# Sums of squares as moving tiles on four column quarters, turned afterwards; one product for the delta layer's two gates, and its key norm ahead of the last convolution

## The reference

```python
# hybrid mixer (layer "ssd"): two norms ahead of its output projection
ssd_out = grouped_rmsnorm(y * silu(z), ssd_norm, 2)        # 2 groups of 512 channels
sc_out  = grouped_rmsnorm(sc, sc_norm, 16)                 # 16 groups of 64 channels
return concatenate([ssd_out, sc_out], axis=-1) @ w_out
# delta rule (layer "gdn"): 4 query heads and 4 key heads of 128 channels
qkv = silu(causal_conv(qkv, conv_w))
q, k, v = split(qkv, [4 * 128, 8 * 128], axis=-1)
q = repeat(l2_norm(q), 2) * 128 ** -0.5;  k = repeat(l2_norm(k), 2)
beta = sigmoid(b);  g = -exp(a_log) * softplus(a + dt_bias)  # a, b: 8 + 8 columns of xn @ w_in
# then chunks of 64 tokens: decays exp(g_i - g_j), inverses of unit lower triangles, a state per head
```

## Time and profile before

| What | Value |
|---|---|
| median of 3 runs | 1317.17 us (1316.4 to 1320.26) |
| profiled execution | 1317.74 us, span 1316.0 us |
| TensorE busy | 1083.5 us, 82% of the span |
| VectorE busy | 638.3 us, 49% |
| ScalarE busy | 438.7 us, 33% |
| GpSimd busy | 8.4 us, 1% |
| chain of waits, by engine | PE 61%, DMA 27%, DVE 5%, ACT 4% |
| mean granted clock of TensorE | 0.944 |
| experts, 250 to 700 us | DMA busy share 1.01, 402 GB/s |

### The profile page before, as it was taken

The page is one execution under the profiler, slowest core; times in us unless marked ns, Lnnn a source line. Parts: engine busy times, 40 slices in busy tenths (PEclk is TensorE's granted clock), DMA queues, the critical chain, the costliest instruction groups (busy, mean ns, idle before and its releaser), DMA issues.

```text
span 1316.0 us, 18871 instructions
## 1 busy us (share of the span) xinstructions
PE 1083.5 (82%) x7678; PEld 792.5 (60%) x7678; DVE 638.3 (49%) x1245; ACT 438.7 (33%) x689; POOL 8.4 (1%) x32
## 2 busy tenths in 40 slices
PE   5999988895656656655656899999989989899998
PEld 5999967731211212121212789887768978778896
DVE  4687387620101010101011877857466975556685
ACT  4554344100000000000001656545345663245563
POOL 1000000000000000000000000000000000000000
PEclk9999899798989898888888999999999999899999
DMA  8655245789999999999998994334413550047700
GB/s 297 200 192 192 90 167 192 272 345 409 409 410 410 410 410 409 410 409 409 410 410 353 230 281 162 129 131 148 170 65 130 193 127 3 1 114 190 220 22 33
DMA packets 120003, 314.63 MB, mean 239 GB/s; under 512 B 17139, under 2 KB 17386, under 8 KB 119674
## 3 DMA queue, kind: packets, MB, share of 16 engines
q1 hardware_dynamic: 116864, 310.78, 65.3%
q0 software_dynamic: 352, 2.11, 0.4%
q10 hardware_dynamic: 2714, 0.71, 0.2%
HBM read 312.52 MB, written 1.06 MB: 238 GB/s over the span
## 4 chain that ended last, share of the span: by engine, by line
PE 61%; DMA 27%; DVE 5%; ACT 4%; issue 1%; SPq 1%; ACTq 0%; DVEq 0%
DMA ring<-in_w_up 17%; DMA ring<-in_w_down 9%; PE bank L2212 7%; PE bank L2205 7%; PE bank L2209 7%; PE bank L2187 6%; PE bank L2191 6%; PE bank L2194 6%; PE bank L2459 5%; PE bank L2480 2%; DMA ring<-in_fox_w_in 1%; PE bank L2121 1%; DVE w_l L1177 1%; PE bank L2446 1%; PE bank L2250 1%
## 5 line engine op out<-in xcount | busy, mean ns | idle before, releaser
L1177 DVE TENSOR_TENSOR w_l<-ring,w_h 128x1024 fp32r<-128x1024 f32 x204 | 246.6, 1221 | 101.3 <-ACT w_h L662 99.8
L662 ACT ACTIVATE w_h<-ring 128x1024 fp32r<-128x1024 f32 x204 | 213.6, 1057 | 193.2 <-PE bank L2194 98.2
L2459 PE MATMUL bank<-ring,cm 128*32 128x512 f32 x960 | 148.2, 749 | 113.4 <-DMA ring<-in_w_up 67.8
L2459 PEld LDWEIGHTS bank<-ring,cm 128*32 128x32 f32 x960 | 29.8, 126 | 225.6 <-DMA ring<-in_w_up 93.2
L2205 PE MATMUL bank<-w_h,hnT_h 128*128 128x512 f32 x480 | 135.0, 403 | 8.5 <-ACT w_h L662 4.7
L2212 PE MATMUL bank<-w_l,hnT_h 128*128 128x512 f32 x480 | 129.9, 393 | 3.7 <-DVE w_l L1177 3.7
L2209 PE MATMUL bank<-w_h,hnT_l 128*128 128x512 f32 x480 | 129.9, 393 | 0.0
L2480 PE MATMUL bank<-ring,cm 128*32 128x512 f32 x496 | 68.8, 693 | 47.5 <-DMA ring<-in_w_down 42.7
L1645 DVE SCALAR_TENSOR_TENSOR cm<-cm,bank 128x512 f32<-128x512 f32 x8 | 5.5, 688 | 209.9 <-ACT cm L871 209.9
L2212 PEld LDWEIGHTS bank<-w_l,hnT_h 128*128 128x128 f32 x480 | 90.2, 189 | 24.9 <-DVE w_l L1177 5.6
L2205 PEld LDWEIGHTS bank<-w_h,hnT_h 128*128 128x128 f32 x480 | 86.8, 189 | 28.3 <-issue 7.6
(11 more groups left out here) (430 smaller groups left out, 1263.6 us busy)
## 6 DMA issues: line engine op xcount, KB each, us to landing
ring<-in_w_down SPq DMA_DIRECT2D x62, 1024.0 KB, 15.8
ring<-in_w_up SPq DMA_DIRECT2D x60, 1024.0 KB, 15.8
ring<-in_w_gate SPq DMA_DIRECT2D x60, 1024.0 KB, 14.7
ring<-in_fox_w_in SPq DMA_DIRECT2D x32, 1024.0 KB, 12.0
ring<-in_w_in SPq DMA_DIRECT2D x22, 1024.0 KB, 8.5
ring<-in_gla_w_in SPq DMA_DIRECT2D x12, 1024.0 KB, 6.3
ring<-in_gdn_w_in SPq DMA_DIRECT2D x12, 1024.0 KB, 6.2
ring<-in_w_out SPq DMA_DIRECT2D x8, 1024.0 KB, 6.4
```

The source lines that it names most:

```text
L662: af(part(w_h, u, width), w, ACT.Copy).then_inc(s["high_ready"], 1)
L1177: v.tensor_tensor(part(w_l, u, width), w, part(w_h, u, width).bitcast(F32), ALU.subtract).then_inc(s["low_ready"], 1)
L2459: x = mm(bank[a][CAP * e:CAP * (e + 1), :], m_xg[:, 2 * b + r, CAP * e:CAP * (e + 1)], expert_of(w, e)[:, r * FF:(r + 1) * FF], start=(b = ...
```

## The change

1. `sum_squares` turns the operands round. The squares move (256 columns), and a one-hot matrix of 32 columns (`whole`, or `halved` with one column for each half of the partitions) is stationary. The four tiles of a group go to the four column quarters of the array, and their sums to 32 partitions each. A row of the result is a head's sums, tokens in the free dimension.
2. VectorE copies the 128x256 result to `sq` (`row_sums`), TensorE transposes it in two pieces (`turn_sums`), and `row_roots` reads the turned sums; for `ssd` a reduction adds four columns first. Counts of `sq_summed` and `rownorm_ready` follow.
3. `sc`: the turn stands behind unit 0 of block 10. VectorE's remainders in this stretch come one step earlier against the pairs.
4. `ssd`: both groups stand behind unit (0, 2), the turn behind unit (0, 3). ScalarE makes the weight part of unit (0, 2) ahead of its wait for the second half of `y`.
5. `gdn`: one product of 16 rows for both gates, and 16-row operations for the second gate's sigmoid. The first group stands behind unit 11, the second behind unit 15, the turn behind unit 19, the spreads behind units 21 and 22. VectorE makes the roots ahead of the last convolution and multiplies two pairs after each of that convolution's middle taps.
6. GpSimd fills the two small matrices in place of selecting them.

```diff
+            def row_sums(name):
+                dve.wait_ge(s["sq_summed"], SUMS_OF[name] + 2)
+                v.tensor_copy(sq[:, 0, 0, :], bank[SUM_OF.get(name, SUM_BANK)][:, 0:T]).then_inc(s["rownorm_ready"], 1)
...
             low(UNIT_BASE["ssd"] + UNITS * 10 + 1)
+            row_sums("sc")
+            low(UNIT_BASE["ssd"] + UNITS * 10 + 2)
             row_roots("sc", 16, 1.0 / 64)
...
             for b in range(4):
-                low(UNIT_BASE["ssd"] + UNITS * 10 + b + 2)
+                low(UNIT_BASE["ssd"] + UNITS * 10 + b + 3 if b < 3 else UNIT_BASE["ssd_out"] + 1)
                 sc_pair(b)
...
             for k in range(2):
+                if k:
+                    high(first + 2 * UNITS + 3)
                 act.wait_ge(s["ssd_yready"], k + 1)
...
+            row_sums("ssd")
             low(first + 3 * UNITS + 1)
             row_roots("ssd", 2, 1.0 / BLK)
...
-                for k in (1, 2, 3):
+                for k in (1, 2):
+                    gdn_copies(k)
                     gdn_conv(k)
+                row_sums("gdn_qk")
                 dve.wait_ge(s["gdn_last"], 1)
                 v.tensor_tensor(tok[:, 4, 0:8], bank[5][:, T + 32:T + 40], tok[:, 0, 0:8],
                                 ALU.subtract).then_inc(s["gdn_col_step"], 1)
-                row_roots("gdn_qk", 8, 1.0)
-                low(UNIT_BASE["gdn_out"] + PARTS - 1)
-                rownorm("gdn_qk", 8, 1.0, qk_out, roots=False)
-                dve.sem_inc(s["gdn_qk_ready"], 1)
+                gdn_copies(3)
+                row_roots("gdn_qk", 8, 1.0)
+                gdn_conv(3, qk_pairs)
+                dve.wait_ge(s["spread_used"], SPREAD_USED["gdn_qk"] + SPREAD_PAIRS["gdn_qk"])
+                dve.sem_inc(s["gdn_qk_ready"], 1)
+                low(UNIT_BASE["gdn_out"] + PARTS - 1)
...
-                    for t in range(NT):
-                        x = mm(bank[SUM_OF.get(name, SUM_BANK)][:, t * R:(t + 1) * R], sq[:, g % 2, i % 4, t * P:(t + 1) * P], pick(i),
-                               start=(i == 0 and t == 0), stop=(i == n - 1 and t == NT - 1), skip_group_check=True)
+            def sum_squares(name, select, u):
+                g = 2 * ROWN[name][0] + u
+                pe.wait_ge(s["sq_ready"], g + 1)
+                for j in range(4):
+                    x = mm(bank[SUM_OF.get(name, SUM_BANK)][32 * j:32 * j + 32, 0:T], select[:, u, :], sq[:, g % 2, j, :],
+                           start=(u == 0), stop=(u == 1), tile_position=(0, 32 * j), skip_group_check=True)
+                x.then_inc(s["sq_summed"], 1)
+            def turn_sums(name):
+                pe.wait_ge(s["rownorm_ready"], 2 * ROWN[name][0] + 1)
+                for t in range(NT):
+                    x = tr(bank[SUM_OF.get(name, SUM_BANK)][:, T + t * P:T + (t + 1) * P], sq[:, 0, 0, t * P:(t + 1) * P], ident[:])
+                x.then_inc(s["sq_summed"], 1)
...
-                small("gdn", [(bank[5][0:8, 0:T], slice(0, 8)), (bank[5][0:8, T:2 * T], slice(8, 16))])
+                small("gdn", [(bank[5][0:16, 0:T], slice(0, 16))])
...
                 project("gdn", 2, 3)
+                pe.wait_ge(s["rbc_ready"], LATE.index("gdn") + 1)
+                sum_squares("gdn_qk", whole, 0)
...
                 project("gdn", 3, 4)
-                sum_squares("gdn_qk", 8, lambda i: column(i, 8), [0])
-                project("gdn", 4, 5)
-                sum_squares("gdn_qk", 8, lambda i: column(i, 8), [1])
-                project("gdn", 5, 6)
-                spread("gdn_qk", 8, lambda i: [i])
+                sum_squares("gdn_qk", whole, 1)
+                project("gdn", 4, 5, lambda m: m == 3 and turn_sums("gdn_qk"))
+                project("gdn", 5, 6, lambda m: m in (1, 2) and spread("gdn_qk", 8, lambda i: [2 * (i % 4) + i // 4], [2 * m - 2, 2 * m - 1]))
```

More of the change, by code:

```diff
@@ L132 @@
 SUM_OF = {"sc": 5}
+SUMS_OF = {"sc": 0, "ssd": 3, "gdn_qk": 6}
 SC_OUT_BANKS = ((4, 5), (6, 7))
@@ L1237, in row_roots @@
                 n = NT * R
[L1238 to L1251, removed]
-                        i = 2 * b + j
-                        x = use(i, b2(6 + g % 2)[:, (i // share) % 2, :])
-                    x.then_inc(s["spread_used"], 1)
-                    if split and b:
-                        out_low(split[0], split[1] + b - 1, tiles(split[2] + 2 * b - 2, 2))
-                if split:
-                    out_low(split[0], split[1] + n // 2 - 1, tiles(split[2] + n - 2, 2))
-                dve.wait_ge(s["spread_used"], SPREAD_USED[name] + SPREAD_PAIRS[name])
+                turned = bank[SUM_OF.get(name, SUM_BANK)][:, T:2 * T]
@@ L1329, in add_projection, with conv @@
                     x_lows(following, (2, 3))
-            def conv(src, dst, weights, stride, taps, bias=None, units=0, first=None):
+            def conv(src, dst, weights, stride, taps, bias=None, units=0, first=None, between=None):
                 n = len(src)
@@ L1352, in conv, with conv_lin @@
                         low(min(n_low[0] + 1, units))
+                        if between is not None:
+                            between(d)
                 return x
-            def conv_lin(k, t0, weights, stride, bias, units, turned, first=None):
+            def conv_lin(k, t0, weights, stride, bias, units, turned, first=None, between=None):
                 lin = [vtm[:, 0, i * T:(i + 1) * T] for i in range(4)]
@@ L1359, in conv_lin @@
                     dve.wait_ge(s["ssd_conv_done"], k)
-                conv([cm[:, t0 + i, :] for i in range(4)], lin, weights, stride, 4, bias, units, first).then_inc(s["lin_ready"], 1)
+                conv([cm[:, t0 + i, :] for i in range(4)], lin, weights, stride, 4, bias, units, first, between).then_inc(s["lin_ready"], 1)
                 low(turned)
@@ L2334, in _, with sc_norm @@
             project("ssd", 4, 10)
[L2335 to L2336 removed]
+            for u in (0, 1):
+                sum_squares("sc", halved, u)
+            def sc_norm(m):
+                if m == 0:
+                    turn_sums("sc")
+                else:
+                    spread("sc", 16, lambda i: [4 * (i % 4) + 2 * (i // 4) + h for h in (0, 1)], [m - 1] if m < 3 else [2, 3])
+            project("ssd", 10, 11, sc_norm)
             pe.wait_ge(s["ssd_conv_done"], 3)
@@ L2410, in _ @@
                                PAIR_BASE["ssd"] + 4 + m + 1 if n == 0 else None, (4 * g, 4 * g + 3))
+                    if n == 0 and m == 2:
+                        for k in (0, 1):
+                            sum_squares("ssd", whole, k)
                 if n == 0:
-                    sum_squares("ssd", 2, lambda i: column(i // 4, 2))
+                    turn_sums("ssd")
             u = NORMS.index("moe")
```

84 lines of the change are left out of this document (47 added, 37 removed).

## The result

The changed kernel takes 1308.01 us (median of 22 runs, 1304.68 to 1316.78) beside 1317.44 us for the kernel before (22 runs, 1313.96 to 1321.26): ratio 0.9932, 95% interval 0.992 to 0.9944. It is faster by 7.4 to 10.5 us; forecast were 8.4 us and 1308.8 us. The profiled execution took 1306.59 us, its span is 1304.9 us. One profile is a sample of one execution. Ten more kernels (e1 to e10) were run, and most of their code is the same; so the stages are compared over all of them further down.

What follows compares the result with a forecast made beforehand. The expert middle hangs on weight transfers whose first releases hang on TensorE, so front gains reach the end. Terms -5.7 - 3.8 + 1.1 = -8.4 us take 1317.74 to 1309.3, as median 1308.8 us; range 1304.3 to 1313.0.

Steps and rivals of the forecast that it cites:

- Price of the sums: All three norms: a new group of sums takes 0.6 us, upper bound 1.7 us if the quarters ran one after the other.
- The prediction's other reading of that row: Expert products on the same quarters: the row shows overlap, with 0.43 us for a product of 512 columns.
- The 0.2 us for each of six groups: Tiling-mode drain going in and out of each group of sums: at most 1.2 us worse in sum.
- sc, forecast -5.7: Short convolution's norm: VectorE's multiply at 160.1 instead of 165.78 us at full clock; bounds -6.3 and -3.5 us.
- one of the two signs by which the prediction calls itself wrong: Changed profile: clock windows staying below 1; the other sign is the delta layer's silu over 9 us earlier.
- the clock falls anyway: TensorE's idling in sc halves the clock for a unit and a half, 1.8 us; gdn up to 0.7; 1311.3 us; chance 0.22.
- ssd, forecast -3.8: State-space norm: TensorE gains 4.5 us, VectorE's last add 0.7 us less; bounds -4.5 and -1.5 us.
- The weight part: State-space layer: ScalarE's 0.95 us part moved ahead of its wait; 0.8 us gained, since a pass then waits for VectorE.
- gdn, forecast +1.1: Delta layer: next stage starts at 1075.8 instead of 1074.66 us, since VectorE doesn't keep up; bounds -2.7 and +3 us.
- One of the signs named: Changed profile: TensorE idle for over 1.5 us ahead of the delta layer's first spread.
- the delta layer delivers: Delta layer: next stage starts up to 2.7 us earlier instead of 1.1 later; 1305.0 us; chance 0.15.
- the slower one: Delta layer's inverses: thin products no longer raise the clock after longer idling and double, 20.8 us; 1329 us; chance 0.04.

Runs made afterwards that it cites:

- e1: Changed kernel with the delta layer's roots, spreads and multiplies behind the last convolution again: gdn 68.68 us, 4.23 shorter; median 2.9 us under the changed kernel.
- e10: Changed kernel with only the eight key and query multiplies behind the delta layer's last convolution, roots still ahead: gdn 71.72 us (72.91 in the changed kernel).
- e9: Kernel before with only ScalarE's weight part of the state-space output moved ahead of its wait: ssd 72.09 us, 1.85 shorter; ratio 0.9993.
- e2: Changed kernel with four unread products in TensorE's wait between the short convolution's groups of sums: sc 20.55 us, 1.49 shorter; median 1.3 us lower.
- e8: Kernel before with four unread products between the short convolution's groups of sums: sc 23.81 us, 2.5 shorter; ssd 75.52 us, 1.6 longer.
- e3: Kernel before with only the delta layer's merged gate product (16 rows, 16-row operations): gdn 69.18 us, 2.72 shorter; ratio 0.9972.
- e4: Changed kernel with the short convolution's second sums, turn and spreads moved later, behind further units: sc 18.59 us, 3.45 shorter; median 2.1 us lower.
- e7: Changed kernel with ScalarE's weight part behind its wait again in the state-space layer: ssd 72.60 us, 2.3 more.
- e6: Changed kernel with sums on two column halves (64-column stationaries) instead of four quarters: ssd 0.92 us longer; median 1.1 us above the changed kernel's.

## Why the prediction was right, step by step

- **Price of the sums.** 0.6 us a group was forecast: 0.57 in the chain where the clock is full, and 1.00 us for two groups. So eight more records cost 0.43 us, the figure that the earlier trace rows gave, and a start is 0.14. (The prediction's other reading of that row, 0.43 us for a product of 512 columns, is wrong: 128 records are 64 products, 0.22 us each. Nothing in its sum used it.) The turn is 0.22 to 0.23 (forecast 0.3). The drain of the Trainium skill (TensorEngine Tiling (Array Packing), Tiling Modes) does not show beside other starts: going in costs at most the 0.14 us, and behind a group the second pass of the next unit starts 1.03 us after the first (217.60 and 218.63 us in the changed kernel), as behind the untiled thin sums of e9 (227.50 and 228.53). The 0.2 us for each of six groups, which the prediction weighed as a price of the drain, are not there on top of the start.
- **sc, forecast -5.7.** It is -4.3 in the profile. The order of steps was right: e2, in which the clock holds, has 20.55 us from first sums to multiply, and the prediction's own steps give 160.1 less 139.54, 20.6 us. What failed is the assumption of a full clock: the window shows 0.76, and a clock window that stays below 1 is one of the two signs by which the prediction calls itself wrong. The rival "the clock falls anyway" happened here, for 1.5 us against its 1.8 (its words, a unit and a half at half clock, would be 4.5 us by its own 3.0 us a unit; in the trace two passes were slow). The prediction's row against that rival, TensorE idle from 203 to 205 us at a clock of 1.00, was a lucky draw: behind this same wait the clock fell in six of twelve kernels, the changed one among them. The rival did not decide the outcome, because before had lost 3.2 us to the same cause (e8): of the 4.3 us, 2.5 are structure (23.81 less the filling's 0.7, less 20.55) and 1.8 are clock. The trace agrees with the Trainium skill's rule (TensorE: Matmul & The Clock Gate, Part 1) that activity is what releases the clock: filling the wait kept it at 1.00 from 142 to 149 us in both kernels.
- **ssd, forecast -3.8.** It is -3.6 in the profile and in every kernel with this code (the six above). Sums -2.47 (forecast -2.3), turn 0.23, roots 2.4 us as worked out, no fall behind the sums (-1.7 forecast; before, two passes take 1.71 and 1.55 us that take 0.91 now). That the new sums are what keeps the clock up there is argued, not shown: e9 has no fall either, with the old sums. The weight part was priced by its wait alone; taken out, it costs 2.3 us.
- **gdn, forecast +1.1.** It is +1.0, and its parts were right too: gate product -2.72 for -2.77; silu 7.4 us earlier, though TensorE ends its last unit 12.3 us earlier (1056.7 instead of 1069.0), because VectorE is late; the silu to the multiply 8.58 us for 8.7. The wait for the turned sums was forecast at 0.4 and is 0.81. One of the signs named did not come: TensorE has no wait ahead of the first spread (VectorE's roots are done at 1046.4 us, the spread starts at 1049.3); its idle time lies behind its last unit, 5.3 us ahead of the products of keys. Behind it the clock is 0.66 from 1062 to 1066 us, which the silu-to-multiply time doesn't show. The rival "the delta layer delivers" and the slower one, in which the thin inverses keep the low clock, did not occur: the inverses take 1.97 us for 32 records at 1069.18, as in the earlier trace rows, after 3.0 us of idling, and the clock is 1.00 from 1075 us on.
- **The sum.** The three stages together give -4.3 - 3.6 + 1.0 = -6.9 us, the times of the runs -9.4 (by the interval -7.4 to -10.5), the two profiles -11.1. The stretches whose code is the same make up most of the difference between stages and profiles: from the last add to the small product they take 760.7 us after and 763.1 before, and over the twelve kernels 760.7 to 766.5 us without a pattern. From the delta layer's multiply to the end it is 238.8 after and 241.3 before, over all kernels 238.8 to 242.6. So the agreement of 1308.0 with 1308.8 us is partly luck: sc missed by 1.4 us, and 2.5 us of gain by the medians (0.5 to 3.6 by the interval) are in no stage. With the luckier clock of e3 in the old code sc would have gained only 2.6 us and still more would be missing. That part stays open.

## What to carry to other kernels

Before shortening a piece of work on an engine, look at what stands behind it: here the first group's saving became a wait of 2.07 us, filling that wait gave back the clock (e2), and only moving the second group behind a unit (e4) turned the wait itself into time. Work moved "ahead" gains only if its engine is not the one that the next stage hangs on: VectorE was, and the key norm ahead of its convolution cost 4.2 us, most of it hidden by 2.7 and 0.5 us gained elsewhere in the layer. Judge the parts of such a change one by one, by lengths between the same marks in the profile; the time of the whole hides a losing part.

## What the runs showed of the hardware

- A wait of TensorE can cost up to 1.7 times its own length: 2.07 us idle ahead of the second sums went with 1.5 us of slow work behind, 1.87 us in e7 with 1.2. Four unread products in the wait took the loss away (e2), and in e8 one of 3.2 us.
- It is not strict: 1.61 us of waiting (e6) and 1.84 us (before, state-space layer: the pass behind takes 1.17) went without a fall right behind, and behind one and the same wait of 2.42 us the clock fell in six kernels of twelve. In e8 the clock fell in a stretch of thin products with no more than 0.34 us of idling in the 14 us ahead.
- Products of 32 stationary columns on four column quarters take 0.43 us for eight records of 256 columns in single precision; with 64 columns on two halves it is twice that (2.00 against 1.07 us for 16 records, in the timeline), and on the whole array eight such records take 1.99 us.
